# Moving weight splits, a key scaling and a gate behind or ahead of other work in a program that streams its weights (one core, two transformer blocks)

## What is computed

```python
# first_block, for l in 0, 1
x = x + 0.5 * swiglu(rms_norm(x, ffa_norm[l]), ffa_w_in[l], ffa_w_out[l])
h = rms_norm(x, mix_norm[l])
(c_q, c_kv, k_rope, g_q, g_k, g_v, g_b, g_a, g_z, m_qkv, gate_logits) = split_cols(h @ w_in[l], IN_SPLITS)
# three branches: latent attention, gated delta rule (its output times silu(g_z)),
# block attention (q and k of m_qkv are rms-normed per head: that is where L1830/L1832 stand)
x = x + jnp.sum(gates * up, axis=2) @ w_out[l]
x = x + 0.5 * swiglu(rms_norm(x, ffb_norm[l]), ffb_w_in[l], ffb_w_out[l])

# second_block, layer 0: even_mixer + conv_glu_ffn; layer 1: odd_mixer + conv_glu_ffn
y_sc = sc_b * causal_dwconv_2(sc_c * sc_x, sc_conv_w)
u = causal_dwconv_2(cf_a * sigmoid(cf_g), cf_conv_w) + cf_conv_b      # 31 taps
u = silu(layernorm(u, cf_ln_g, cf_ln_b))
even = concatenate([y_sc, u]) @ w_out
y_lru = rg_lru(xc, ...) * gelu(lru_gate)                              # a scan over 256 tokens
y_att = dilated_attention(rmsnorm(q), rmsnorm(k), v)                  # 3 groups of 4 heads
odd = concatenate([y_lru, y_att]) @ w_out
ffn = (silu(causal_dwconv_2(h @ w_gate, conv_w) + conv_b) * (h @ w_up)) @ w_down
```

## Time and profile before

| | |
|---|---|
| median of 3 runs | 1899.18 us (1899.68, 1897.37, 1899.18) |
| the profiled execution's own time | 1898.54 us |
| its span in the trace | 1896.7 us |
| TensorE busy / VectorE / ScalarE / GpSimd | 100% / 77% / 57% / 4% of the span |
| granted TensorE clock | 1.0 |
| moved from the chip's memory | 327.91 MB, 174 GB/s over the span |

### The profile page before, as it was taken

One profiled execution on the slowest core, in us unless ns is written; L12 is line 12 of the kernel. 1 busy time (PEld: TensorE's weight loads), 2 busy tenths in 40 slices (PEclk: granted clock), 3 DMA queues, 4 the chain that ended last, 5 costly groups with the idle time before them and its releaser, 6 DMA issues.

```text
span 1896.7 us, 32369 instructions
## 1 busy us (share of the span) xinstructions
PE 1888.9 (100%) x11791; PEld 1649.9 (87%) x11791; DVE 1459.9 (77%) x2316; ACT 1083.9 (57%) x1681; POOL 82.5 (4%) x61
## 2 busy tenths in 40 slices
PE   9999999999999999999999999999999999999999
PEld 9888998788988888889987888889888889888888
DVE  7777896877777777778777777777578888888887
ACT  6555764664555555467647645555346555675654
POOL 0000011010000000000110010000000000110000
PEclk9999999999999999999999999999999999999999
DMA  6666563445455555555534455555755665544654
GB/s 237 196 191 197 171 188 102 134 148 172 157 188 188 189 180 196 189 178 189 154 113 146 145 167 179 192 188 189 207 179 169 196 196 170 167 145 158 199 187 143
DMA packets 116717, 330.87 MB, mean 174 GB/s; under 512 B 10896, under 2 KB 40208, under 8 KB 116496
## 3 DMA queue, kind: packets, MB, share of 16 engines
q1 hardware_dynamic: 114496, 325.64, 53.8%
q10 hardware_dynamic: 2128, 3.94, 0.6%
HBM read 327.91 MB, written 1.64 MB: 174 GB/s over the span
## 4 chain that ended last, share of the span: by engine, by line
PE 94%; DVE 3%; ACT 2%; DMA 1%; issue 0%; POOL 0%; ACTq 0%
PE ps L2316 90%; DVE w_lo L1318 1%; PE ps L2342 1%; DMA raw<-stream 1%; ACT w_hi L615 1%; PE ps L2615 1%; PE ps L2865 0%; DVE sc L1830 0%; DVE arena L2131 0%; PE ps L3029 0%; PE ps L2806 0%; PE ps L2887 0%; PE ps L3001 0%; ACT gates L1112 0%; PE ps L2686 0%
## 5 line engine op out<-in xcount | busy, mean ns | idle before, releaser
L1318 DVE TENSOR_TENSOR w_lo<-raw,w_hi 128x1024 fp32r<-128x1024 f32 x614 | 750.2, 1228 | 220.6 <-ACT w_hi L615 219.2
L2316 PE MATMUL ps<-w_hi,a_both 128*128 128x512 f32 (+2 forms) x2368 | 753.2, 387 | 1.2 <-DVE a_both L2103 0.9
L615 ACT ACTIVATE w_hi<-raw 128x1024 fp32r<-128x1024 f32 x614 | 637.6, 1053 | 153.4 <-DMA raw<-stream 98.3
L2316 PE MATMUL ps<-a_both,w_hi 128*128 128x256 f32 (+1 forms) x3360 | 712.6, 342 | 0.0
L2316 PEld LDWEIGHTS ps<-a_both,w_hi 128*128 128x128 f32 x3360 | 580.7, 190 | 72.9 <-issue 0.8
L2316 PEld LDWEIGHTS ps<-w_hi,a_both 128*128 128x128 f32 x2368 | 441.9, 188 | 88.8 <-DVE a_both L2103 1.3
L2316 PE MATMUL ps<-w_lo,a_both 128*128 128x512 f32 (+2 forms) x1184 | 455.4, 385 | 0.0
L2316 PE MATMUL ps<-a_both,w_lo 128*128 128x256 f32 x2592 | 448.1, 283 | 0.0
L2316 PEld LDWEIGHTS ps<-a_both,w_lo 128*128 128x128 f32 x2592 | 380.5, 191 | 8.9
L2316 PEld LDWEIGHTS ps<-w_lo,a_both 128*128 128x128 f32 x1184 | 223.2, 188 | 36.5
L688 ACT ACTIVATE a_both<-arena 128x256 fp32r<-128x256 f32 x132 | 55.2, 418 | 139.1 <-DVE arena L1432 98.3
(11 more groups left out here) (348 smaller groups left out, 1185.1 us busy)
## 6 DMA issues: line engine op xcount, KB each, us to landing
raw<-stream SPq DMA_DIRECT2D x613, 512.0 KB, 3.6
arena<-upad SPq DMA_DIRECT2D x8, 284.0 KB, 6.4
gates<-late ACTq DMA_DIRECT2D x1, 1088.0 KB, 7.1
out<-tmp SPq DMA_DIRECT2D x3, 256.0 KB, 2.3
upad<-arena ACTq DMA_DIRECT2D x2, 288.0 KB, 7.4
con<-consts SPq DMA_DIRECT2D x1, 560.0 KB, 5.2
raw<-stream ACTq DMA_DIRECT2D x1, 512.0 KB, 3.7
x<-x_in ACTq DMA_DIRECT2D x2, 256.0 KB, 5.2
```

Source lines behind the costliest of these rows:

```text
L615: nc.scalar.activation(laid(w_hi, u), loaded(u), ACT.Copy).then_inc(hi_ready, 1)
L1318: V.tensor_tensor(laid(w_lo, u), loaded(u), laid(w_hi, u), ALU.subtract).then_inc(split_ready, 1)
L2316: return nc.tensor.matmul(o, a, b, start=start, stop=stop, **k)
```

## The change

Four orders are changed, on VectorE and ScalarE; the same instructions are issued in another order.

```diff
                 split(b0 + 2 + AHEAD); split(b0 + 3 + AHEAD)
                 ysc_high(1)
-                split(e0 + AHEAD); split(e0 + 1 + AHEAD)
+                split(e0 + AHEAD)
                 for p in range(2):
                     act.wait_ge(*DV2.at(0, f"yb{p}"))
                     nc.scalar.activation(flat(lnth[:, 2 * p:2 * p + 2, :]), flat(cf[:, 2 * p:2 * p + 2, :]), ACT.Tanh
                                          ).then_inc(*AC2.sig(0, f"lnth{p}"))
-                split(e0 + 2 + AHEAD)
                 for p in range(2):
                     act.wait_ge(*DV2.at(0, f"o2_{p}"))
...
-                for k in range(3, 8):
+                for k in range(1, 8):
                     split(e0 + k + AHEAD)
...
                 if conv:
                     split(three(FT - 1)[1] + AHEAD)
-                split(n0 + 3 * FT - 3 + AHEAD)
+                else:
+                    split(n0 + 3 * FT - 3 + AHEAD)
...
                         for q, r in enumerate((sA, sB)):
+                            if q:
+                                z_gate(1)
                             link(V.tensor_reduce(sc[:, 160 + 16 * q:176 + 16 * q], r.rearrange("p (a b) -> p a b", b=MD),
                                                  AX.X, ALU.add))
...
                     moba_step(m)
-                    if m == 2:
-                        z_gate(1)
...
-                split(e0 + AHEAD)
-                split(e0 + 1 + AHEAD)
                 for p in range(2):
                     dve.wait_ge(*AC2.at(0, f"lnth{p}"))
...
-                for k in range(2, 7):
+                for k in range(7):
                     split(POS["ev_out"] + k + AHEAD)
...
-                for i in range(4):
-                    scan = tick(V.tensor_tensor_scan(tqb[:, i, :], aa[:, i, :], thi[:, i, :], 0.0, ALU.mult, ALU.add))
                 dve.wait_ge(*PO2.at(0, "drsk"))
                 for j in range(TT):
                     r = dil["k"][:, j, :].rearrange("p (a b) -> p a b", b=DD)
                     e = V.tensor_tensor(r, r, over(drs["k"][:, 12 * j:12 * j + 12], DD), ALU.mult)
                 e.then_inc(*DV2.sig(0, "dk"))
+                for i in range(4):
+                    scan = tick(V.tensor_tensor_scan(tqb[:, i, :], aa[:, i, :], thi[:, i, :], 0.0, ALU.mult, ALU.add))
                 split(d0 + 9 + AHEAD)
...
                 if i == 0:
-                    update(t, POS["ffn", i] + 3 * FT, 1.0, ("mix2", 1))
+                    update(t, POS["ffn", i] + 3 * FT, 1.0, ("mix2", 1), between=POS["ffn", i] + 3 * FT - 3 + AHEAD)
```

## The result

The changed kernel takes **1903.29 us** (median of 12 runs, 1901.82 to 1906.07) against 1899.15 us before (12 runs, 1897.37 to 1900.06). The ratio is 1.0024, with a 95% interval of 1.0016 to 1.0032: 4.1 us slower, clear of no change. The prediction was 1903.1.

The account below looks back on a forecast made before the run. TensorE was taken as the bound, busy 1888.9 of 1896.7 us. Terms 1.6 - 0.5 + 1.2 + 1.65 = 3.95 us slower took 1898.54 to 1902.5, plus 0.64 for the median: 1903.1, range 1898.8 to 1905.0.

Parts of the forecast that it names:

- forecast case: Whole kernel: three of the four edits lose more than they win, median 1903.1 us; chance 0.40.
- the sum of 3.95: Whole kernel: conv stage, first conv FFN, odd stage and mixer terms together, 3.95 us slower.
- Conv stage, gain: Conv stage: TensorE no longer waits for the low part of o2, 1.1 us won.
- loss by the transposes: Behind the conv stage: late load 453 delays the x updates TensorE's transposes need; net 1.6 us slower, gain included.
- End of the FFN: End of first conv FFN: split goes behind the updates, transposes start sooner, 0.5 us faster (bounds 0.3 and 0.7).
- Odd stage: Odd stage: keys turned 0.8 us sooner, but VectorE stands still 1.6 us; net 1.2 us slower.
- the first turning: Odd stage: normalised probabilities come 1.6 us late where TensorE turns them, cover 0.43 us; new wait about 2 us.
- Mixer: Both mixer layers: a split starts ahead of GpSimd's mask and holds it, 0.8 us per layer, 1.65 us slower together.
- The first rival: Mixer: mask starts ahead of the split, term -0.2 instead of +1.65, time 1901.3 us; chance 0.27.
- The fourth rival: Late loads collide, late queries hold TensorE: conv +2.4, odd +1.6, mixer +2.0, sum +5.5, 1904.7 us; chance 0.09.
- second and third rivals: Second: conv stage's cover holds, 1900.4 us, chance 0.15. Third: VectorE's late work absorbed everywhere, 1896.4 us, chance 0.09.

Follow-up runs that it names:

- a_only: Kernel before with only the conv stage's new order on ScalarE and VectorE: 1900.73 us against 1898.14, ratio 1.0013.
- b_only: Kernel before with only the split moved behind the updates in the first conv FFN: 1897.62 us against 1898.14, ratio 0.9997.
- c_only: Kernel before with only the key scaling moved ahead of all four scans: 1899.50 us against 1898.14, ratio 1.0006.
- d_only: Kernel before with only the z gate moved ahead of the second reduction, both layers: 1899.97 us against 1898.14, ratio 1.0007.
- c_three: Kernel before with only the key scaling moved, behind three of the four scans: 1898.03 us against 1898.67, ratio 0.9996.
- d_behind: Kernel before with the z gate as changed and the next step's split behind the next matrix (L1870): 1898.58 us against 1898.67, ratio 1.0001.
- conv_one: As a_only, but on VectorE only the split of 448 moved, that of 447 staying ahead of o2: 1898.91 us against 1898.71 before, ratio 1.0003.
- a_filled: As a_only, plus 22 small unread products on TensorE during its wait for the update of x: 1901.60 us against 1898.71 before, ratio 1.0017.
- all_mended: All four edits, with split 453 behind the x updates, scaling behind three scans, mixer split behind L1870: 1897.64 us against 1898.67 before, ratio 0.9994.

## Why the prediction was right, point by point

The forecast case came in, at 1903.29 for 1903.1, and the signs and places of its terms hold. That it fits to 0.2 us is luck: the sum has no term for the clock, and the median lies between the runs with and those without a fallen clock. In the six runs without it the kernel is 3.0 us slower than before, 1.0 less than the sum of 3.95; in the six with it, 5.3. Why those without it lose less than the steps of the profiled execution add up to (4.1, below) is not shown. They may be the ones in which load 453 lands sooner, so that the wait is shorter and the clock holds.

- *Conv stage, gain* 1.1: 1.19 in the changed kernel and in a_only. Right. In the five profiles whose conv stage is as before (b_only, c_only, d_only, c_three, d_behind) the same place steps by -0.15 or -0.16, since the wait there was 0.2 us longer than theirs in the old kernel's profile; so about 1.0 of the 1.19 is the edit's.
- *Conv stage, loss by the transposes*, net +1.6: 1.76 and 1.72. The chain of loads was right in each link; conv_one, which puts load 453 back in its place, confirms it.
- *Conv stage, what the sum left out*: the granted clock after the wait, 1.6 us in both profiled executions with the order as changed. The median of a_only is only 2.6 us above before, not 3.3, and the clocks on record show that not every run pays it: the mean clock is below 1.000 in four of 11 runs there (median 1902.0 against 1900.3) and in six of 12 of the changed kernel (1904.4 against 1902.1).
- *End of the FFN*, -0.5: -0.65, and -0.65 alone. Right, within its bounds. The load it makes late had cover.
- *Odd stage*, +1.2: +1.25, and +1.40 alone. The sum was right. Two terms were not as put: the keys are turned 0.5 to 0.6 us sooner, not 0.8, and the sentence that the loss comes all at the first turning missed ScalarE's list, in which L1094 stands behind the split that waits for load 541. So the loss came in two waits.
- *Mixer*, +0.8 per layer: +0.79, all four masks (two layers, two kernels) long. The first rival, the mask ahead of the split, was given 0.27; it didn't happen. The rule of the Trainium skill was cited for this place: SBUF — State Buffer, the section on the two sides. The mask agrees (2.19 us behind a split, 1.30 alone).
- *Sum*: the steps of the profiled execution's difference give 6.6 us, of which 0.7 (`upad`) and 0.2 (start) are at places that the change doesn't touch and 1.6 are the clock; what is left, 4.1, is what was forecast (3.95). The fourth rival's +2.0 for the mixer has no row behind it; the mixer's own upper figure was 1.65. The medians of the four parts alone, +2.6, -0.5, +1.4 and +1.8, sum to 5.3 rather than to the 4.1 of the whole; each has an interval of about 1.7 us to either side, so that this can't be taken for an interplay. One small one is seen: TensorE's wait for the scaled keys takes up what TensorE is late by (step -1.18 there in a_filled, -0.30 in a_only).

The second and third rivals (covers that hold) fail by the transposes' wait of 2.8 us and the probabilities' of 0.7. The page Perfetto Trace Analysis of the Trainium skill advises to find the contended engine's gaps and have what they wait for start sooner. All four gaps did shrink or vanish, and the kernel is slower all the same: in the conv stage the work that had to make room was feeding a chain of loads, in the odd stage VectorE stood still and made such a chain late, and in the mixer the mask met a split.

## What to carry to other kernels

Where an in-order engine both computes results and frees the buffers of a stream, moving a result ahead of a "free" step is paid three units later, at whatever stands behind the late unit in any engine's list. Follow the load that the moved step releases until its unit is split, on each engine that handles it, and look at what waits in line behind; if it is a result, move the late step behind that too. And work that waits for another engine belongs where that engine's answer has just come: the scaling behind three scans won 0.7 us in the trace, where the scaling ahead of all four lost 1.4.

## What the hardware showed that was not expected

- **A stall of TensorE can cost more than its length.** In both profiled executions with a wait of 2.8 us the granted clock fell to 0.50, in one 1.3 us behind the wait's end (after), in the other already within it, 0.2 us before its end (a_only). It stayed there for 3.4 us, and 1.6 us were lost in addition. In the profiled executions it did not fall after waits of 1.3 us (conv_one), 1.7 us (all_mended) or 0.9 us (d_only), nor when the same stretch was filled with products that nobody reads (a_filled). A mean clock below 1.000 is on record for six of 12 and four of 11 runs of these two versions, against three of 121 runs of the eleven other versions and two of 99 of the kernel before. The Trainium skill has the mechanism (TensorE: Matmul & The Clock Gate, the part on the clock gate: the array's rate is halved after it has been idle, and how this falls out varies between runs); the traces agree, 0.50 being 1.2 of 2.4 GHz, and so do the runs with and without the fall.
- **VectorE and GpSimd exclude each other in both directions.** A mask of 1.30 us takes 2.2 when a split has begun 0.14 to 0.17 us before it; a split of 1.22 takes 1.75 when the mask was first. But a power of 5.43 us on GpSimd holds no VectorE instruction that starts within it: in the changed kernel it runs from 303.84, and the split of this row starts within it and takes its usual time.

```profile
304.21 1.22 DVE L1317 TENSOR_TENSOR w_lo<-raw,w_hi 128x1024 fp32r<-128x1024 f32 x1
```
